# A two-block transformer kernel on one core: norm vectors loaded apart, and the order of copies, queries, best keys, slot gates, zeros and exit turning changed

## The reference

```python
h = rmsnorm(x, norm_g[i]); mem_h = rmsnorm(mem, mem_norm_g[i])
proj = h @ w_in                      # q, k, v (three dilations in layer A), q_mem, gate
o_mix = mixer_dilated(...) if i % 2 == 0 else mixer_axial_gqa(...)
  # dilated: three windows; shares = softmax over the three log-sum-exps; o = sum(share * o_g)
o_mem = memory_attention(q_mem, mem_h, w_mem_kv[i], ...)
x = x + (concat([o_mix, o_mem]) * silu(gate)) @ w_out[i]
```

```python
h = x @ w_in[l]
o_a = sliding_window_sink_attn(...)   # 8 heads, window 128
o_b = indexer_sparse_attn(...)        # the best 64 keys of each token, by top_k of indexer scores
q_c = rms_norm(c_q) @ w_uq[l]; kv_c = rms_norm(c_kv) @ w_ukv[l]; o_c = mla_attn(...)
x = layer_norm(alpha * x + concat([o_a, o_b, o_c]) @ w_out[l], ln1_g[l], ln1_b[l])
x = layer_norm(alpha * x + moe_ffn(x, w_router, ...), ln2_g[l], ln2_b[l])
  # 16 experts in 4 groups, 2 per token, gates from sigmoid scores
```

## Time and profile before

| | us |
|---|---|
| three runs | 1166.01, 1168.52, 1171.72 (median 1168.52) |
| the profiled execution | 1168.65 |
| its span | 1167.2 |
| TensorE busy | 1117.7 (96%), 5515 instructions |
| TensorE weight load busy | 914.2 (78%) |
| VectorE busy | 895.2 (77%) |
| ScalarE busy | 741.7 (64%) |
| DMA | 221.25 MB, mean 190 GB/s |

### The profile page before, as it was taken

The page is one execution under the profiler, slowest core; times in us unless marked ns, Lnnn a source line. Parts: engine busy times, 40 slices in busy tenths (PEclk is TensorE's granted clock), DMA queues, the critical chain, the costliest instruction groups (busy, mean ns, idle before and its releaser), DMA issues.

```text
span 1167.2 us, 14667 instructions
## 1 busy us (share of the span) xinstructions
PE 1117.7 (96%) x5515; PEld 914.2 (78%) x5515; DVE 895.2 (77%) x1462; ACT 741.7 (64%) x1313; POOL 0.2 (0%) x4
## 2 busy tenths in 40 slices
PE   7999999999999999998999999999989999999996
PEld 5788787888787788887877787877778778787774
DVE  4756857777768867766668868999977886899996
ACT  5746565655656665556355556888845655688883
POOL 0000000000000000000000000000000000000000
PEclk9999999999999999999999998999999999999998
DMA  8654454453443455633542416999926322499991
GB/s 288 239 181 144 145 177 137 157 179 109 145 140 114 164 197 172 201 108 106 184 145 108 145 38 190 348 360 359 360 91 214 130 99 87 157 357 357 364 349 39
DMA packets 131841, 221.25 MB, mean 190 GB/s; under 512 B 6144, under 2 KB 77360, under 8 KB 131760
## 3 DMA queue, kind: packets, MB, share of 16 engines
q1 hardware_dynamic: 127920, 213.21, 53.2%
q10 hardware_dynamic: 3840, 6.98, 1.8%
HBM read 219.13 MB, written 1.05 MB: 189 GB/s over the span
## 4 chain that ended last, share of the span: by engine, by line
PE 74%; DVE 14%; ACT 7%; issue 3%; DMA 2%; ACTq 0%; DVEq 0%
PE bank L487 20%; PE bank L489 20%; PE bank L488 20%; PE bank L786 3%; PE bank L851 3%; DVE wL L440 2%; ACT wH L432 2%; ACT S L806 2%; DMA ring<-in_w_mem_kv 1%; PE bank L636 1%; PE bank L2277 1%; PE bank L832 1%; DVE mx L795 1%; PE bank L2326 1%; PE bank L1738 1%
## 5 line engine op out<-in xcount | busy, mean ns | idle before, releaser
L440 DVE TENSOR_TENSOR wL<-ring,wH 128x1024 fp32r<-128x1024 f32 (+1 forms) x316 | 375.9, 1213 | 138.5 <-ACT wH L432 137.3
L432 ACT ACTIVATE wH<-ring 128x1024 fp32r<-128x1024 f32 (+1 forms) x316 | 320.5, 1047 | 32.3 <-PE bank L489 19.8
L487 PE MATMUL bank<-wH,hTH 128*128 128x512 f32 (+2 forms) x592 | 237.9, 402 | 3.0 <-DVE wL L440 2.1
L488 PE MATMUL bank<-wL,hTH 128*128 128x512 f32 (+2 forms) x592 | 232.1, 392 | 0.0
L489 PE MATMUL bank<-wH,hTL 128*128 128x512 f32 (+2 forms) x592 | 231.9, 392 | 0.0
L487 PEld LDWEIGHTS bank<-wH,hTH 128*128 128x128 f32 x592 | 111.5, 188 | 27.9 <-DVE wL L440 3.5
L489 PEld LDWEIGHTS bank<-wH,hTL 128*128 128x128 f32 x592 | 111.5, 188 | 24.8
L488 PEld LDWEIGHTS bank<-wL,hTH 128*128 128x128 f32 x592 | 111.6, 189 | 23.1 <-issue 0.5
L487 PE MATMUL bank<-wH,xgH 128*128 128x512 f32 x256 | 105.2, 411 | 0.0
L488 PE MATMUL bank<-wL,xgH 128*128 128x512 f32 x256 | 101.9, 398 | 0.0
L489 PE MATMUL bank<-wH,xgL 128*128 128x512 f32 x256 | 101.9, 398 | 0.0
(11 more groups left out here) (297 smaller groups left out, 1863.0 us busy)
## 6 DMA issues: line engine op xcount, KB each, us to landing
ring<-in_w_in_a SPq DMA_DIRECT2D x44, 1024.0 KB, 4.9
ring<-in_w_out SPq DMA_DIRECT2D x20, 1024.0 KB, 4.8
ring<-in_w_down SPq DMA_DIRECT2D x20, 1024.0 KB, 6.3
ring<-in_w_gate SPq DMA_DIRECT2D x36, 512.0 KB, 5.1
ring<-in_w_up SPq DMA_DIRECT2D x36, 512.0 KB, 6.5
ring<-in_w_in_b SPq DMA_DIRECT2D x14, 1024.0 KB, 5.0
ring<-in_w_mem_kv SPq DMA_DIRECT2D x8, 1024.0 KB, 7.1
ring<-in_w_in SPq DMA_DIRECT2D x8, 1024.0 KB, 5.4
```

The source lines that it names most:

```text
L432: act.e.activation(quarter_parts(q)[0], quarter_in_ring(q), COPY).then_inc(w_high, 1)
L440: dve.e.tensor_tensor(lo, quarter_in_ring(q), hi.bitcast(F32), SUB).then_inc(w_low, 1)
L487: pe.e.matmul(o, a[0], b[0], start=first, stop=False)
L488: pe.e.matmul(o, a[0], b[1], start=False, stop=False)
```

## The change

- The start: `mem_norm_g` is the second small transfer, and the first wait is for it and the constants only. The other two vectors go to rows 32 to 63 of `grow`, have a semaphore of their own, and are turned by a product of their own behind the second `ahead` of the memory weights, in a bank taken from the four, and copied by ScalarE (`gcol 2`) behind `act_ahead(4)`.
- Layer A: the rotation tables are made in two steps, at n = 0 and n = 4; for u = 5 the gated flips and their copies stand ahead of one quarter of the gates' weights; the second part of the shares on ScalarE moves from n = 2 to n = 4, with the weight quarters moved too.
- Layer B: at n = 11 the output's flips' copies stand ahead of the weight cuts.
- Block 2: `second_tile` of the second layer stands in front of tile 1 (`place` (1, 0)) and no longer in front of chunk 6 of tile 0; the queries' `qT3` flips come after unit 4; the best keys' rounds of tile 1 are one at a time where they were two; more products of zeros; the slot gates are made in four pieces, at experts 0, 4, 8 and 12.

```diff
@@ pe_proj_by_tiles
-        def pe_proj_by_tiles(name, meanwhile):
+        def pe_proj_by_tiles(name, meanwhile, place):
                 for kk in range(8):
-                    if i == 0 and kk == 6:
+                    if (i, kk) == place:
                         meanwhile()
@@ act_first_loads, pe_layer_a
             act.e.dma_start(const[:, 0:keep], t["const"][:, 0:keep]).then_inc(d_id, 16)
-            act.e.dma_start(grow[0:16, :], t["norm_g"].rearrange("l (k p) -> (l k) p", p=P)).then_inc(d_id, 16)
-            act.e.dma_start(grow[16:32, :], t["mem_norm_g"].rearrange("l (k p) -> (l k) p", p=P)).then_inc(d_id, 16)
-            act.e.dma_start(grow[32:48, :], t["ln1_b_2"].rearrange("l (k p) -> (l k) p", p=P)).then_inc(d_id, 16)
+            act.e.dma_start(grow[0:16, :], t["mem_norm_g"].rearrange("l (k p) -> (l k) p", p=P)).then_inc(d_id, 16)
+            act.e.dma_start(grow[32:48, :], t["norm_g"].rearrange("l (k p) -> (l k) p", p=P)).then_inc(d_gain, 16)
+            act.e.dma_start(grow[48:64, :], t["ln1_b_2"].rearrange("l (k p) -> (l k) p", p=P)).then_inc(d_gain, 16)
-            pe.wait_ge((d_id, 64))
+            pe.wait_ge((d_id, 32))
             pe_ahead(2)
             pe_ahead(4)
+            b = att_bank(("gains 2",), at("gcol 2"))
+            pe.wait_ge((d_gain, 32))
+            pe.e.transpose(b.t[:, 0:32], grow[32:64, :], ident[32:64, 32:64]).then_inc(*pe.did("gains 2"))
             pe_flip(("hT", "A"), chunk(T0), 8, [(d_x0, 64)])
                 if u == 5:
+                    pe_gated("o0", 0, OUT_ORDER)
                     pe_ahead(1)
-                    pe_gated("o0", 0, OUT_ORDER)
@@ act_layer_a
             act_ahead(4)
-            act_flip_high(("hT", "A"), 8, hT[0], gcol[:, 0:8])
+            act.wait_ge(at("gains 2"))
+            act.e.activation(gcol[:, 16:48], bank_of["gains 2",].t[:, 0:32], COPY).then_inc(*act.did("gcol 2"))
+            act.wait_ge(at("gcol 2"))
+            act_flip_high(("hT", "A"), 8, hT[0], gcol[:, 16:24])
                     def between(n):
-                        if n in (0, 2):
-                            act_shares(n // 2)
-                        act_ahead(1 - n % 2)
+                        if n in (0, 4):
+                            act_shares(n // 4)
+                        act_ahead({0: 1, 4: 2}.get(n, 0))
@@ dve_layer_a
-                        if u < 2 and n == 2:
-                            dve_tables(2 * u + 2, "cA", "sA", 16, [f"qa{u + 1}", f"ka{u + 1}"])
+                        if u < 2 and n in (0, 4):
+                            dve_tables(2 * u + 2 + n // 4, "cA", "sA", 16, ["qk"[n // 4] + f"a{u + 1}"])
@@ layer B, VectorE, between(n)
+                if n == 11:
+                    dve_flip_y("o1", 4, 4)
+                    dve_upto("o12", 8)
                 dve_ahead(1 if n in (0, 1, 9, 12) else 2)
-                if n == 11:
-                    dve_flip_y("o1", 4, 4)
-                    dve_upto("o12", 8)
@@ block 2
-            pe_proj_by_tiles(f"h{l}0", second_tile)
+            pe_proj_by_tiles(f"h{l}0", second_tile, (1, 0) if l else (0, 6))
             def between(n):
                 pe_ahead(1)
-                if n == 3:
+                if n == 4:
                     pe_flip(("qT3", l), chunk(HR), 4, [at("queries", l)])
-            pe_idle(12, att_bank(("idle", l, 2), None))
+            pe_idle(14, att_bank(("idle", l, 2), None))
-            pe_idle(5, att_bank(("idle", l, 3), None))
+            pe_idle(8, att_bank(("idle", l, 3), None))
                 if 0 < n < 5:
-                    best(1, 2)
+                    best(1, 2 if n == 4 else 1)
...
+                if n in (3, 5, 7):
+                    best(1, 1)
@@ pe_few, dve_few
-            def slot_gates():
-                b = att_bank((*way, "gates"), at(*way, "slot_gate"))
+            def slot_gates(g):
+                b = att_bank((*way, "gates", g), at(*way, "slot_gate", g))
                 pe.wait_ge(at(*way, "gates"))
-                for g in range(4):
-                    for i in range(2):
-                        mm = pe.e.matmul(b.t[:, 4 * g:4 * g + 4], OH[:, i, g * P:(g + 1) * P].bitcast(F32), SG[:, i, 4 * g:4 * g + 4], start=i == 0, stop=i == 1)
+                for i in range(2):
+                    mm = pe.e.matmul(b.t[:, 0:4], OH[:, i, g * P:(g + 1) * P].bitcast(F32), SG[:, i, 4 * g:4 * g + 4], start=i == 0, stop=i == 1)
+                if e % 4 == 0:
+                    slot_gates(g)
                 if e:
                     down(e - 1)
-                else:
-                    slot_gates()
             if l == 0:
-                pe_idle(10, att_bank((*way, "idle"), None))
+                pe_idle(14, att_bank((*way, "idle"), None))
```

45 lines of the change are left out of this document (25 added, 20 removed).

## The result

The change made the kernel slower by 1.4%: ratio 1.0143, 95% interval 1.0111 to 1.0175. Four executions took 1178.58 to 1188.34 us (median 1186.8), those of the kernel before on the same chip 1167.35 us in the median. The forecast was 1170.0 us. The profiled execution of the change took 1185.27 us with a span of 1183.8, 16.6 us more than before. In what follows one execution each of the kernels `no_exit` and `no_mix` is left out (1393.4 and 1408.5 us, at a mean granted clock of 0.75 and 0.74): it lies far off the other nine of its kernel.

What follows compares the result with a forecast made beforehand. TensorE, busy 96% of the span, was taken as the bound. From 1168.65 us, ten points summed to +3.05 us and the clock to −1.7, giving 1170.0 us; stated range 1163.0 to 1175.5.

Steps and rivals of the forecast that it cites:

- the clock: TensorE's half-clock stretches: two go (−3.4), idle pieces at start, shares and exit add one (+1.7), net −1.7 us.
- rival B: Idle stretches at start, shares and exit each end in half clock; 1176.9 us, chance 0.16.
- Start: Kernel start: earlier first wait is swallowed by a new wait for `gcol 2`; +0.3 us (−0.4 to +1.7).
- Tables: Layer A, 121 us: rotation tables in two steps close a 1.45 us wait for `PT`; −1.3 us.
- gated flips: Layer A, u = 5, 350 us: a weight quarter covers most of a 1.16 us gap; −1.0 us.
- layer B: Layer B: flips in front shorten a 1.28 us wait for `PT`, two weight cuts still ahead; −0.2 us.
- zeros: First exit and both layers: added zero products fit under idle gaps; 0 us (up to +1.9).
- slot gates: Experts' part: gates by group save 0.7 but add three times 0.45 us; +0.65 per layer, +1.3 us.
- Shares: Layer A, 379 us: the 2.48 us gap moves behind VectorE's later queue and does not close; +2.15 us.
- Exit: Layer 1 exit: second tile's flips and products lie open behind chunks 6 and 7; +3.2 us (+2.4 to +5).
- Later flips: Mix layers: `qT3` flips one unit later, most returns in the wait for VectorE's rotations; −0.2 each, −0.4 us.
- Best keys: Mix layers: spread rounds shorten four waits for the normalising by 0.25 us each; −1.0 us.

Runs made afterwards that it cites:

- no_exit: The whole change with its exit turning taken back (second tile's flips and router product in front of chunk 6 again): 1177.3 us, ratio 1.0054.
- no_mix: The whole change without the later `qT3` flips and without the spread of the best keys' rounds: 1174.4 us, ratio 1.0058.
- only_exit: The kernel before with only the exit turning moved in front of tile 1: 1169.2 us, ratio 0.9998.
- only_shares: The kernel before with only the shares' edit on ScalarE (second part after the last probabilities' copy): 1172.4 us, ratio 1.0013.
- only_best: The kernel before with only the best keys' rounds spread out: 1169.4 us, ratio 1.0009.
- the saving parts: The kernel before with tables in two steps, gated flips ahead, layer B's flips, more zeros and slot gates by group: ratios 0.9959 and 0.9972 in two comparisons.
- exit_zeros: The kernel before with the exit turning plus 18 products of zeros in front of chunk 6 of tile 0: 1175.9 us, ratio 1.0055.
- shift7: The kernel before with only seven products of zeros after the first unit of layer A: 1169.4 us, ratio 1.0010.
- no_qT3: The whole change without the later `qT3` flips: 1177.9 us, ratio 1.0094.
- zeros_slots: The kernel before with only more products of zeros and the slot gates by group: 1168.4 us, ratio 1.0015.
- head_mended: The kernel before with only the norm vectors' edit, ScalarE's second gains' copy behind one weight quarter, no longer four: 1170.0 us, ratio 1.0002.
- good_again: Second comparison, in more rounds, of the kernel before with tables, gated flips, layer B's flips, zeros and slot gates: 1164.4 us, ratio 0.9972.

## Why the prediction was wrong, point by point

**The step that failed is the clock.** It took away two stretches (−3.4), added one (+1.7), and each was priced at 3.4 us of half clock, the length they had in the trace of before. Its term was −1.7 us. Measured is 17.5 us more loss, which is an estimated 12 us of time; by the busy time in the two profiles it is at most 16.4. Three things were wrong in it.

- *The length.* The stretches of the change are 6.8 to 13.7 us. At half clock the narrow products and turnings take longer, as at the exit (3.43 for 1.86 us), and in this profile the clock did not come back while they ran. In `only_exit` it did, in the middle of the turnings, after 6.8 us.
- *The number.* I priced one new stretch for three idle pieces of about 5 us; all three had one. That none of them alone costs measurable loss (shares +1.7, start −0.3, exit −2.6) was not known, and would have supported my number.
- *The mix layers.* I saw that the later flips gave nothing at full clock, and did not ask what their wait in one piece does to the clock. Two stretches of 10.2 us, nearly half of all half clock, stand there. They cost about 3.4 us each.

The prediction's rival B had the mechanism (idle stretches at start, shares and exit end in half clock) with a chance of 0.16 and a price that was too low: 1176.9 us, outside of the stated range and 10 us under the measured time. It lacked the mix layers, and the falls at 702 and 720 us that it kept did go. Two slips of its arithmetic change nothing of this: B's words say "+1.7 twice" where its sum adds it once, and the range's "−4 to +5 about the forecast" gives 1166.0 to 1175.0, not the 1163.0 to 1175.5 that are stated.

**Of the rule of the Trainium skill** that idle gaps in the middle of a kernel bring the clock to half ("TensorE: Matmul & The Clock Gate", section "Why this matters for your kernels") the prediction said that all three long stretches would fall by it. They did, in both profiles of the change. Filling them took 15 us of the mean loss away. But at the start 3.4 us of half clock also stood in the profiles of `only_shares` and `only_best`, which have the start of before and where TensorE waited only 2.3 and 2.4 us ahead of the quarter at 33.23 us. (In the profile of before this wait was 0.30 us: the same instructions wait differently from one execution to the next.) The rule alone does not tell of the mix layers, where the fall came behind a wait of only 1.3 us among narrow products and turnings, and in no_mix behind one of 0.99.

**The sum at full clock** was +3.05 us. Measured is +4.7 at equal loss, so the sum was about right. The parts alone, taken at equal loss, add up to the same: −0.2 (start), +2.3 (shares), +3.0 (exit), +0.8 (later flips), +1.4 (best keys) and −2.0 to −2.7 (the saving parts), together 4.6 to 5.3, each with an error of about 0.5. By its points, as measured:

1. *Start:* +0.3, measured alone −0.1. Right; the wait for `gcol 2` came as described, and TensorE's first wait is 5.4 us long.
2. *Tables, 3. gated flips, 5. layer B, 9. zeros, 10. slot gates:* −1.2 together, measured −0.9 and −2.2 in the two runs. Right as a sum; the zeros and slot gates alone measured 0.0 where +1.3 was forecast. The wait at 121 us and the gap at 350 us are gone.
4. *Shares:* +2.15, measured +1.8 (2.3). Right, with the wait moved to where the prediction put it.
6. *Exit:* +3.2, measured alone +3.8 (3.0). Right.
7. *Later flips:* −0.4, measured −0.9, but +0.8 at equal loss, so that no gain is shown; and the loss of 5.6 us was not in it.
8. *Best keys:* −1.0, measured +1.6. Wrong in sign. The wait of 0.86 us did shrink, to 0.24, but the next wait for the normalising grew from 0.61 to 1.19 us: VectorE now does three rounds between the two weight cuts ahead of it, where it did two. The weight cuts behind each mix layer come 0.4 us later. First the kernel before, then `only_best`:

```profile
968.06 0.63 PE L943 MATMUL bank<-const,Y 128*128 128x128 f32 x4 [0.61 <-DVE Y L858]
```

```profile
951.06 0.66 PE L943 MATMUL bank<-const,Y 128*128 128x128 f32 x4 [0.24 <-DVE Y L858]
...
966.41 0.92 PE L943 MATMUL bank<-const,Y 128*128 128x128 f32 x4 [1.19 <-DVE Y L858]
```

Of the signs that the prediction named, these came true: no wait at 121 us, the shares' first operation on VectorE near 378 us (377.83 in the change) with a wait of over 4 us behind it, chunk 6 with the flips behind it at the exit, the quarters of the start about 2.5 us later. Not true was the latent chain 3 us later: it came 7 us later in the change, half clock included, but 3.3 us with the exit's edit alone. And half clock in more than three stretches was named as what would make it wrong.

**What stays open.** The losses of the parts do not add up. Alone, the edits change the loss by −0.3 (start), +1.7 (shares), −2.6 (exit), +5.6 (later flips), −0.6 (best keys) and −1.5 to −3.7 (the saving parts), in sum about 1 us, with an error of about 3; together by 17. Why together they bring so much more isn't known. The clock in the twenty profiles, one execution each, tells which stretches go with an edit:

- *Shares.* The six profiles with the shares' edit and no zeros there have 6.8 or 10.2 us of half clock between 382 and 394 us. The fourteen others have 3.4 us or none.
- *Experts' part, 703 and 720 us.* The eleven kernels with more zeros and the slot gates by group have neither stretch. But four of the nine without have neither too (`only_exit`, `exit_zeros`, `only_best`, `shift7`), and `only_exit` has no edit ahead of 860 us. So one profile without them proves little.
- *Exit.* 13.7 us in the whole change, 6.8 in `only_exit` and 3.4 in `no_qT3`, all with the same order there; 6.8 in `no_exit` and `zeros_slots`, with the order of before.
- *Mix layers.* Stretches of 10.2 or 13.7 us also fell in kernels that do not touch the place: in the first in `no_mix`, `head_mended`, `zeros_slots` and `good_again`, in the second in `zeros_slots` and `exit_zeros`. The kernel before did not fall there in its profile, but lost 14 us or more in 33 of 140 executions.

It isn't settled what besides the instructions at a place, its waits and a plain shift in time decides. What is shown is that filling idle pieces takes most of the additional loss of the whole change away in the mean (27.5 to 12.7 us), at a price of full-clock time, and that leaving out the later flips or the exit turning takes 7 to 9 us each.

## What to carry to other kernels

Where the profile shows a few short stretches of half clock, price every edit twice: by the queue, and by the idle and narrow pieces that it leaves on TensorE. Here an edit that joined two short waits into one longer wait was nearly free at full clock and brought 5.6 us of loss. Split each execution into span times clock and the rest before comparing kernels, and check on executions of one kernel what a microsecond of the rest is worth in time (0.7 here). Some 12 of the 17 us were in the second part, and parts tested alone did not show it. Take more than one profile before calling a stretch gone or new: the falls changed from one execution to the next.

## What the runs showed of the hardware that was not expected

- Half clock began within TensorE's idle time (0.52 in the stretch from 880 to 882 us of the change) and lasted for 13.7 us while TensorE was busy for 12.0 of them, with turnings and products of 16 columns in the middle. With the same order of work it lasted 3.4 us in `no_qT3`.

```profile
880.00:882.00 2.00, 0.25 (x1) 0.25 (x2) 1.02 (x1) 0.17 (x1) 0.00 (x0) 0.52 0.01 4
```

- The same kernel differs between executions by up to 13 us (1164.8 to 1177.6), and this goes with the loss (4.7 to 23.5 us): the full-clock time scatters by 1.2 to 1.7 us only (standard deviation in the five sets).
- Half clock can cost less than half of the time that TensorE is busy in it: in the mix layers of the change, 3.4 us for a stretch of 10.2 us in which TensorE was busy throughout.
- Products of zeros, 0.23 us each (4.09 us for 18), put into a wait of 4.83 us: the clock was 1.00 there in the profiled execution.
